# A transformer block on one core: additions, seams and the order of passes

## The reference

```python
h = rmsnorm(x, norm_mix_g)
proj = h @ w_in                       # mixer A: sliding-window attention, mixer B: stick-breaking attention
y_a, y_b = o_a @ w_branch_a, o_b @ w_branch_b
gates = sigmoid(h @ w_gate + b_gate)
x = x + (gates[0] * y_a + gates[1] * y_b) @ w_out
x = x + cross_attention(rmsnorm(x, norm_cross_g), rmsnorm(mem, norm_mem_g), w_xq, w_xkv, w_xo)
hf = rmsnorm(x, norm_ffn_g)
g, u = split(hf @ w_gu)               # 5632 columns each
x = x + (silu(g) * u) @ w_down
return rmsnorm(x, final_norm_g)
```

## Time and profile before

| | us |
|---|---|
| median of 3 runs | 2825.31 (2821.89 to 2825.94) |
| profiled execution | 2823.73 |
| its span | 2821.8 |
| PE busy | 2731.7 |
| DVE busy | 1717.8 |
| ACT busy | 1018.3 |
| POOL busy | 771.8 |
| mean granted TensorE clock | 0.993 |

### The profile page before, as it was taken

One profiled execution on the slowest core, in us unless ns is written; L12 is line 12 of the kernel. 1 busy time (PEld: TensorE's weight loads), 2 busy tenths in 40 slices (PEclk: granted clock), 3 DMA queues, 4 the chain that ended last, 5 costly groups with the idle time before them and its releaser, 6 DMA issues.

```text
span 2821.8 us, 35057 instructions
## 1 busy us (share of the span) xinstructions
PE 2731.7 (97%) x13710; PEld 2285.7 (81%) x13710; DVE 1717.8 (61%) x1904; ACT 1018.3 (36%) x1134; POOL 771.8 (27%) x642
## 2 busy tenths in 40 slices
PE   9999999999999999999999999999999989999997
PEld 7888888888788888896777888888888877777776
DVE  6667643345633353663767767676767666666666
ACT  6545532225632231343623333333333322222224
POOL 0000000000000003500366666666666621313130
PEclk9999999999999999999999999999999999999999
DMA  6222233332233352342333343434444464343432
GB/s 239 68 89 74 67 101 97 97 97 83 68 97 97 97 187 90 97 150 74 105 125 107 127 134 128 135 128 134 129 133 130 132 224 150 119 149 118 151 116 82
DMA packets 115138, 333.30 MB, mean 118 GB/s; under 512 B 10320, under 2 KB 43088, under 8 KB 114384
## 3 DMA queue, kind: packets, MB, share of 16 engines
q1 hardware_dynamic: 108544, 309.37, 33.8%
q10 hardware_dynamic: 6480, 22.35, 1.9%
HBM read 301.27 MB, written 30.41 MB: 118 GB/s over the span
## 4 chain that ended last, share of the span: by engine, by line
PE 75%; DVE 18%; ACT 3%; issue 3%; DMA 1%; POOL 0%; SPq 0%; DVEq 0%; ACTq 0%
PE acc L1795 14%; PE acc L1797 14%; PE acc L1796 14%; PE ps L2169 9%; PE acc L1822 4%; PE ps L2170 4%; PE acc L1824 4%; PE acc L1823 4%; DVE w_lo L1585 2%; PE acc L2169 2%; DVE cg L1613 2%; DVE cg L1614 2%; DVE cu L1613 2%; DVE cu L1614 2%; DVE w_lo L1098 2%
## 5 line engine op out<-in xcount | busy, mean ns | idle before, releaser
L1098 DVE TENSOR_TENSOR w_lo<-raw,w_hi 128x1024 fp32r<-128x1024 f32 x328 | 456.5, 1397 | 287.1 <-ACT w_hi L610 286.6
L1795 PE MATMUL acc<-act_both,w_hi 128*128 128x512 f32 (+1 forms) x1536 | 591.5, 385 | 5.9 <-DVE w_lo L1098 4.5
L1797 PE MATMUL acc<-act_both,w_lo 128*128 128x512 f32 (+1 forms) x1536 | 585.4, 381 | 0.0
L1796 PE MATMUL acc<-act_both,w_hi 128*128 128x512 f32 (+1 forms) x1536 | 585.2, 381 | 0.0
L610 ACT ACTIVATE w_hi<-raw 128x1024 fp32r<-128x1024 f32 x328 | 344.4, 1054 | 599.0 <-PE acc L1797 343.0
L1795 PEld LDWEIGHTS acc<-act_both,w_hi 128*128 128x128 f32 x1536 | 289.6, 189 | 62.6 <-issue 6.0
L1797 PEld LDWEIGHTS acc<-act_both,w_lo 128*128 128x128 f32 x1536 | 289.4, 188 | 55.6
L1796 PEld LDWEIGHTS acc<-act_both,w_hi 128*128 128x128 f32 x1536 | 289.6, 189 | 54.7 <-issue 0.7
L2169 PE MATMUL ps<-t_both,w_hi 128*128 128x512 f32 x896 | 325.9, 398 | 0.0
L1822 PE MATMUL acc<-act_both,w_hi 128*128 128x512 f32 x672 | 265.5, 395 | 33.9 <-DVE x L1453 27.2
L544 POOL MEMSET mem_stat<- 128x256 f32 x1 | 0.3, 311 | 1048.1 <-DMA mem<-mem_t 1048.1
(11 more groups left out here) (299 smaller groups left out, 4909.8 us busy)
## 6 DMA issues: line engine op xcount, KB each, us to landing
raw<-w_stream SPq DMA_DIRECT2D x440, 512.0 KB, 3.6
over<-w_stream SPq DMA_DIRECT2D x56, 512.0 KB, 4.1
gate_t<-cg ACTq DMA_DIRECT2D x22, 512.0 KB, 2.6
over<-gate_t SPq DMA_DIRECT2D x22, 512.0 KB, 5.0
up_t<-cu ACTq DMA_DIRECT2D x20, 512.0 KB, 2.6
over<-up_t SPq DMA_DIRECT2D x20, 512.0 KB, 6.2
x<-x_t SPq DMA_DIRECT2D x16, 512.0 KB, 8.5
x_tokens<-x_n SPq DMA_DIRECT2D x4, 1024.0 KB, 15.5
```

The costliest lines, as they stand in the source:

```text
L1098: nc.vector.tensor_tensor(w_lo[:, s, :], raw[:, s, :], f(w_hi[:, s, :]), ALU.subtract)\
L1795: nc.tensor.matmul(dst, wh, ah, start=start and k == 0, stop=False)
L1796: nc.tensor.matmul(dst, wh, al, start=False, stop=False)
L1797: last = nc.tensor.matmul(dst, wl, ah, start=False, stop=stop and k == UK - 1)
```

## The change

It has six parts.

1. **Down projection.** DVE's work for the next group goes between the two additions of one `down`: one operation each at n = 1 to 6 (gate parts at 1 and 3, up parts at 2 and 4, low parts at 5 and 6). ACT's order follows: two conversions, a sigmoid, two conversions, a sigmoid, one, a high part, one, a high part, two. ACT's wait for the last stores to DRAM moves from before the stage into the sigmoid.
2. **Cross output stage.** DVE converts after the even addition and `x_low`, not before them.
3. **Start of the mixed groups.** DVE converts a unit between the halves of `mixed_low`, and takes the reciprocal after the first mixed unit.
4. **A fourth raw buffer** for mixed units, in `over_hi`; the load of unit n waits for the low part of unit n - 4 in place of n - 3.
5. **Order of passes.** Per product and unit PE runs both wide passes and then both narrow ones, where it was wide, narrow, wide, narrow.
6. **Seam into the down projection.** SP loads the first four units of the stage before the stretches of `x` that come back, and one unit earlier; ACT converts the first unit before the hidden tiles; DVE converts one unit before the low parts of the hidden tiles, one inside the last `read_products` (`between`), and one after it; the second `acc` bank is waited for by the first step of the last readout.

```diff
@@ SP, mixed loads and seam
-                else:
-                    sp.wait_ge(lo_done, U_MIX + (-2, 0)[n] if n < 2 else U_MIX + n - 2)
+                elif n != 3:
+                    sp.wait_ge(lo_done, U_MIX + (-2, 0)[n] if n < 2 else U_MIX + n - 3)
...
-                sp.wait_ge(lo_done, U_DOWN - 2 if n < 2 else U_DOWN - 1 if n < 4 else U_DOWN + n - RING + 1)
+                sp.wait_ge(lo_done, U_DOWN - 3 if n < 2 else U_DOWN - 2 if n < 4 else U_DOWN + n - RING + 1)
...
+            for n in range(4):
+                late_weights(n)
             for c in range(4):
                 sp.wait_ge(unit_done, U_DOWN - 3 + c)
                 if c == 1:
                     hidden_in(0)
-                    late_weights(0)
-                    late_weights(1)
-                if c == 2:
-                    late_weights(2)
-                    late_weights(3)
                 x_in_again(c)
@@ mix_raw
-            if n % 3 == 2:
-                return over_lo[:, 0:UK, SH:S]
-            return raw[:, 2 * (n % 3):2 * (n % 3) + 2, :].rearrange("p r (b c) -> p (r b) c", b=4)
+            if n % 4 >= 2:
+                return (over_lo, over_hi)[n % 4 - 2][:, 0:UK, SH:S]
+            return raw[:, 2 * (n % 4):2 * (n % 4) + 2, :].rearrange("p r (b c) -> p (r b) c", b=4)
@@ ACT
                 if last:
                     mix_convert()
+                    convert(1)
                     act.wait_ge(hid_in[0], 32)
...
-                    convert(1)
                     convert(1)
                     convert(2)
...
             def group(slot):
-                units(3)
-                sigmoids(slot)
-                units(3)
-                hidden_high(slot)
                 units(2)
-
-            act.wait_ge(gate_stored, 16 * (MIXES + 1))
-            act.wait_ge(up_stored, 16 * (MIXES - INLINE + 1))
+                sigmoid_high(slot, 0)
+                units(2)
+                sigmoid_high(slot, 2)
+                units()
+                hidden_high(slot, 0)
+                units()
+                hidden_high(slot, 2)
+                units(2)
@@ DVE, cross output stage
             for m in range(KT):
-                if m % 2 == 0:
-                    units()
                 dve.wait_ge(half_done if m % 2 == 0 else unit_done, unit.at(1 - (0 if m % 2 else U_XO)))
                 add_out(m)
                 if m:
                     x_low(act_lo[:, m - 1, :], act_hi[:, m - 1, :], m - 1, G_FFN)
                 if m % 2:
                     unit.add()
+                else:
+                    units()
@@ DVE, start and end of the mixed groups
             mixed_low(0)
-            rstd_of(4, rstd, S)
+            units()
             mixed_low(1)
-            units(2)
+            units()
             unit.add(4 * DIRECT)
             out_no.add(2 * DIRECT)
-            mix_low(5)
+            mix_low()
+            rstd_of(4, rstd, S)
+            mix_low(4)
...
                 if last:
-                    hidden_low(0)
+                    units()
+                    hidden_low(0, 0)
+                    hidden_low(0, 2)
...
-                read_products(2 * p - 1, cu)
+                read_products(2 * p - 1, cu, units if last else lambda: None)
...
                 if last:
-                    units(3)
+                    units()
@@ DVE, read_products and down: between() is called here
                 added(out[:, 3, :], out[:, 2, :], lambda h: half(3, h), freed)
+                between()
                 dve.wait_ge(products_done, len(TOLD) * g + 4)
...
                 add_out(m)
                 if last:
                     add_final_square(m - 1)
+                between()
                 dve.wait_ge(unit_done, unit.at(1))
                 add_out(m + 1)
@@ DVE, middle
+                def next_group(n):
+                    if n == 1:
+                        dve.wait_ge(hid_in[slot], arrived[slot].at(64))
+                        arrived[slot].add(64)
+                    if n in (1, 3):
+                        times_rstd(over_lo, n - 1, gate_scaled)
+                    elif n in (2, 4):
+                        times_rstd(over_hi, n - 2, up_scaled)
+                    elif n in (5, 6):
+                        hidden_low(slot, 2 * (n - 5))
+
                 for n in range(KT // 2):
-                    down(2 * n, first=first)
-                    if n == 2:
...
+                    down(2 * n, first=first, between=lambda: next_group(n))
@@ PE
                     for j in range(2):
-                        src = (act_both if kind == "b" else t_both)[:, :, ks.start + 2 * c + j, toks]
-                        cols = slice(P * j, P * (j + 1))
-                        first, end = c == 0 and j == 0, c == 3 and j == 1
-                        nc.tensor.matmul(dst, hi[:, w_block, cols], src, start=first, stop=False)
-                        last = nc.tensor.matmul(dst[:, SH:S], lo[:, w_block, cols], src[:, 1, :], start=False, stop=end)
+                        nc.tensor.matmul(dst, hi[:, w_block, P * j:P * (j + 1)], src[:, :, ks.start + 2 * c + j, toks],
+                                         start=c == 0 and j == 0, stop=False)
+                    for j in range(2):
+                        last = nc.tensor.matmul(dst[:, SH:S], lo[:, w_block, P * j:P * (j + 1)],
+                                                src[:, 1, ks.start + 2 * c + j, toks], start=False,
+                                                stop=c == 3 and j == 1)
...
-            down(0, split.at(), banks=(READ_STEPS * (2 * MIXES - 2) + 1, READ_STEPS * 2 * MIXES))
+            down(0, split.at(), banks=(READ_STEPS * (2 * MIXES - 2) + 1, READ_STEPS * (2 * MIXES - 1) + 1))
```

60 lines of the change are left out of this document (26 added, 34 removed).

## The result

The changed kernel takes 2775.07 us, the median of four runs (2773.41 to 2777.86); the kernel before took 2823.60 beside it (four runs, 2821.53 to 2825.94). The ratio is 0.9829, 95% interval 0.9812 to 0.9846. The forecast was 2777. Of the 1.9 us between 2777 and 2775.07, 1.7 are the kernel before itself, which the forecast took at 2825.31.

A forecast was written before the change was run, and what follows sets the result against it. TensorE was taken as the limit, with holes made by the order of VectorE's work. Gains 30.4 + 4.5 + 6.2 + 0 + 2.6 + 4.1 = 47.8 us gave 2775.9 profiled, 2777 us as median; range 2766 to 2797.

The forecast's parts named there:

- down projection: Down projection groups: VectorE's work spread between additions cuts the group period from 46.9 to 43.9 us, gaining 30.4 us.
- cross output stage: Cross output stage: conversion hidden behind the even addition, so seven units take 38.1 instead of 42.55 us, gaining 4.5.
- first projections: First FFN projections: the 4.31 us wait for low weights and the half clock after it go, gaining 6.2 us.
- fourth buffer: Mixed stage: loads and sums move one unit earlier, worth 0, with 2 us either way.
- pass order: Mixed stage: two wide then two narrow passes halve the width changes, gaining 2.6 us (ends +5.3 and -3.7).
- seam: Seam into the down projection: second unit 5.8 us earlier, less 1.7 for half clock, gaining 4.1 us.
- The early need of the hidden tiles: Down projection: the first scaling might wait for hidden tiles loaded about 2485 us; costed at nothing.
- the slower pace is a price of changing width: Mixed stage: the 0.353 us pair pace exceeds 0.347, the sum of single-width steps, because pass width changes.
- No nearer to that chain: Mixed stage, fourth buffer: earlier loads and sums come no nearer the second unit's wait behind VectorE's last ten readouts; worth 0.
- Port collisions in the down projection: Rival 1, down projection: one 1.9 us stop a group, 30.4 becomes 15, time 2792 us; chance 0.17.
- Narrow after narrow exposing the weight load: Rival 2, mixed stage: the narrow-to-narrow step exposes the weight load; at 0.227 us it costs 76 us (2855); chance 0.04.
- Seams that don't deliver: Rival 3, seams: another operand ends last and the stages keep their length, 10 us less, 2787 us; chance 0.10.

The follow-up runs named there:

- the second time: The full change measured once more without an edit, against the kernel before: 2775.53 us, ratio 0.9825.
- pairs in turn: Changed kernel with the two pairs of hidden tiles handled one after the other in each down group: 2771.57 us, 0.9814.
- short products: Changed kernel with GpSimd's two products in the down projection cut from 512 tokens to 128: 2772.52 us, a single run.
- in company: Old pass order, or three raw buffers, put back into the changed kernel: 2778.74 us (0.9835) and 2779.61 us (0.9840).
- moved addition: Changed kernel with the down projection's first addition inside the last readout and the third conversion behind the second addition: 2776.59 us, 0.9833.
- the kernel after it: Changed kernel with tile pairs one after the other, first addition inside the last readout, and seam loads in order of need: 2772.14 us, 0.9816.

## Why the prediction came out right, and where it was wrong

The sum was 47.8 us; the medians give 48.5 and, the second time, 49.2. The mechanism held for the three largest terms. That the total comes within 1.4 us is closer than the single terms are, so it is partly luck. Term by term:

| term | predicted | measured |
|---|---|---|
| down projection | 30.4 | 31.4 by medians, 32.2 by stage, alone |
| cross output stage | 4.5 | 4.5 |
| first projections | 6.2 | 6.3 |
| fourth buffer and pass order | 0 + 2.6 | 0.1 and 2.1 by the mixed stage |
| seam | 4.1 | 1.9 to 2.8 (5.2 and 4.5, less 2.4 and 2.6 that the down stage has more than in the kernel with its part alone) |

- **Down projection: right in its mechanism, one time mis-sized.** The unit before the stop began at 2428.78 (23 steps of 0.2267 before 2433.99). From there the prediction had the sigmoid end at 1.2, GpSimd's product at 3.7, VectorE's conversion at 4.8, the addition at 5.45. The rows have 1.3, 3.8, 4.8 and 5.45. Only the deadline was wrong: PE starts 0.05 us after the addition, so the bank need be free at about 5.4, not 5.1. That is 0.16 to 0.17 us in half the groups, 0.25 in the mean, instead of 0.42, 1.7 us less over ten groups. The pairs in turn confirm the link through the late sigmoid; the short products confirm that GpSimd is behind the stop, by the conversion beside the product, the sigmoid, or both. The early need of the hidden tiles cost nothing, as charged: VectorE waited 0.4 us for them in all.
- **Cross output stage and first projections: right.** Seven units take 1369.20 - 1331.12 = 38.08 us; the first mixed matmul is at 1413.63 (1413.5 was named), no half clock before it. The two alone bring 9.9 us of 10.7, and 0.8 is lost by the tenth mixed unit.
- **Pass order: the step "the slower pace is a price of changing width" is refuted.** All unwaited units now run at one pace, 0.348 a pair where 0.350 was expected, between the two of the earlier trace rows, and changing width a seventh as often leaves it there. The premise under it fails too: in runs of one width inside the mixed stage a wide pass takes 0.229 and a narrow one 0.119, not 0.2267 and 0.120, so 0.347, the sum of the latter, isn't what a mixed stream falls to when its width seldom changes. The arithmetic had a slip as well: 2.4 units' gain of four makes 2.8 of 4.6 us, not 2.6. That the new order brings the units to one faster pace was right in direction, and its number, near the 2.0 to 2.5 us in company, was right by accident. Alone it can't be told from none (0.9995), so the reading that the order is worth 0 isn't excluded there; that VectorE's wait passes only part of it on held: the waits grew from 15.7 to 21.2 us. What sets the pace of a mixed stream isn't settled by these runs.
- **Fourth buffer: 0 was right for the buffer alone, wrong in the reason.** "No nearer to that chain" misses both sides. It takes waits away (12.5 us of PE's waits instead of 15.7 alone, 4.1 to 4.5 us in the settled groups between three and four buffers in the full change), and it brings GpSimd's sums beside VectorE's inline products at the front, 0.9 us, the way "when GpSimd's work meets VectorE's" was priced at 2 us. In company its ratio is 0.0011 to 0.0015 better, 3.1 to 4.2 us, with intervals that overlap.
- **Half-clock windows in the mixed stage** were in no term. The forecast left that stage's clock as it was; 3.4 to 13.6 us at 0.50 in its first 21 units can make up to 5 us of difference between executions (half of 10.2, an estimate).
- **Seam: the right wait, half the price back.** The second unit did wait for the first addition, 3.9 us (2275.00 to 2279.14 less one step), where the working had 3.7 and the list of signs said about 5. The clock was then at 0.50 for 3.4 us, as charged (1.7). That window is most of what came back: eight steps in it take 0.43 instead of 0.227, and the first eight units from the second on take 45.6 us against 43.7 to 44.1 in the later groups. The gross gain was 5.2 and 4.5 us of the 5.8 named; where nothing is changed at this seam, the same length is 13.70 to 15.20 us in five kernels, so it isn't known better than that. Here too the clock goes with it: the two longest (15.15 and 15.20) have 10.2 us at 0.50, the three others (13.70 to 14.14) 6.8. Measured from the down projection alone, seam and down stage together (468.13 us there) are only 0.9 to 1.8 us shorter in the full change. The moved addition shows that behind this wait stands the arrival of weights, and the kernel after it that behind the weights stand the sigmoid and GpSimd's product, so that with the first wait gone alone the stage gains little.
- **The rivals.** Port collisions in the down projection: there in every group, but 0.16 to 0.49 us each, not 1.9. Narrow after narrow exposing the weight load: the step is 0.115 us in the changed kernel and 0.118 to 0.119 in runs of fourteen, refuted. Seams that don't deliver: refuted for the first two by their 82.51 us; at the third, removing one wait did bring out the next.

The parts alone make 31.4 + 9.9 + 1.4 + 1.4 = 44.1 us by their ratios (the last two within their error of none), the full change 48.5. The seam, which none of them has, accounts for 1.9 to 2.8 of the difference, or 0.9 to 1.8 against the down projection alone. The other 1.6 to 3.5 us stay open: each ratio is known to 0.001 or 0.0015, 3 to 4 us, so they may be noise, half-clock windows, or what order and buffer bring only together.

## What to carry to other kernels

Where the engine that limits has holes and the one that makes them has slack, list the deadlines of one unit and put each extra operation in a gap of its own; worked out row by row this forecasts a stop of a few tenths of a us. Take a pace from the stream itself and test its cause with one kernel that changes the supposed cause by a large factor, before a number is built on it. A wait removed at a stage's start is worth no more than the distance to the next thing that arrives late: look for the loads, and the other engines' work, behind it first. When two executions of one kernel differ by some us, compare their time at half clock, stage by stage, before a part of the change is given the difference. And where a gap grows, add up its neighbours: it may have swallowed the next one.

## What the runs showed of the hardware

- What GpSimd holds up is VectorE's operation with both inputs in SBUF: the conversion takes 2.59 or 3.10 us beside a product. Sums whose second input is a PSUM bank aren't held, and don't hold GpSimd, whose sum of 128x512 keeps its usual 1.28 to 1.30 us:

```profile
1435.44 0.42 DVE L1612 TENSOR_TENSOR cg<-ps,cg 128x256 f32<-128x256 f32 x1
...
1435.05 1.28 POOL L569 TENSOR_TENSOR over<-over 128x512 f32<-128x512 f32 x1
```

- GpSimd pays for a meeting too: of its sums in the mixed stage, the same one of 128x256 takes 0.74 us or, when it starts beside a conversion, 2.40, ending after it:

```profile
1412.43 0.74 POOL L571 TENSOR_TENSOR raw<-raw 128x256 f32<-128x256 f32 x1
...
1415.32 2.40 POOL L571 TENSOR_TENSOR over<-over 128x256 f32<-128x256 f32 x1
...
1415.01 2.12 DVE L1585 TENSOR_TENSOR w_lo<-raw,w_hi 128x1792 fp32r<-128x1792 f32 x1 [3.28 <-ACT w_hi L952]
```

- A stop of PE costs 0.08 to 0.11 us more than it lasts: the second step after it takes 0.31 to 0.34 us instead of 0.227, the same in the down projection behind stops of 0.05 us as behind stops of 2.48.
- Half-clock windows in the mixed stage stand beside the longest steps between matmuls, but not at the same ones each time. In the profile above stretches at 0.50 begin 1.5 us behind the step of 3.1 us that ends at 1465.4 and inside the one of 3.7 that ends at 1512.7; in its second execution behind the step of 3.5 before 1464.3 alone, though the later one takes 3.4; with the pairs in turn behind the step of 3.0 before 1446.3 and inside the one of 3.2 before 1509.8; in the kernel before behind the step of 3.1 before 1519.7, and not at the equal one before 1474.4.
